# Feed forward's second projection by seven products of quarters, with accumulating transfers, and weights laid out tile by tile

## The reference, cut to what matters

```python
D_FF_2 = 4 * D_MODEL                       # 4096
def rmsnorm(x, g):
    xf = x.astype(jnp.float32)
    xf = xf * lax.rsqrt(jnp.mean(xf * xf, axis=-1, keepdims=True) + EPS)
    return (xf * g.astype(jnp.float32)).astype(x.dtype)

y = rmsnorm(h, pre_ff_g)                   # 512 x 1024
a = jnp.square(jax.nn.relu(y @ w_ff1))     # 512 x 4096, the hidden values
h = h + rmsnorm(a @ w_ff2, post_ff_g)      # 4096 x 1024 weights: the second projection
```

## Time and profile before

| | |
|---|---|
| median of 3 runs | 1729.72 us (1729.71 to 1730.04) |
| the profiled execution's own time | 1730.73 us |
| its span, first to last instruction | 1729.0 us |
| TensorE (PE) busy | 1715.3 us, 99% |
| VectorE (DVE) busy | 1209.1 us, 70% |
| ScalarE (ACT) busy | 820.2 us, 47% |
| GpSimd (POOL) busy | 46.4 us, 3% |
| moved by the 16 DMA engines | 181.36 MB, mean 105 GB/s |

### The profile page before, as it was taken

The page is one execution under the profiler, slowest core; times in us unless marked ns, Lnnn a source line. Parts: engine busy times, 40 slices in busy tenths (PEclk is TensorE's granted clock), DMA queues, the critical chain, the costliest instruction groups (busy, mean ns, idle before and its releaser), DMA issues.

```text
span 1729.0 us, 26320 instructions
## 1 busy us (share of the span) xinstructions
PE 1715.3 (99%) x10458; PEld 1497.2 (87%) x10458; DVE 1209.1 (70%) x1975; ACT 820.2 (47%) x1449; POOL 46.4 (3%) x103
## 2 busy tenths in 40 slices
PE   9999999999999999999999999999999999999998
PEld 8777788999999887777989999989888898999997
DVE  4588787777787735666877777868446876677776
ACT  4477744444445235664444444443565555333342
POOL 0212000000000000000000000000000000000000
PEclk9999999999999999999999999999999999999999
DMA  8343332333334232224133333352314224333331
GB/s 276 113 134 118 119 89 87 109 98 110 101 99 153 86 105 84 81 91 122 39 103 98 110 110 97 99 165 82 110 44 140 63 73 126 106 98 98 100 109 49
DMA packets 220125, 181.36 MB, mean 105 GB/s; under 512 B 9906, under 2 KB 178771, under 8 KB 220003
## 3 DMA queue, kind: packets, MB, share of 16 engines
q1 hardware_dynamic: 217954, 175.48, 33.1%
q0 software_dynamic: 2048, 4.20, 0.9%
HBM read 173.32 MB, written 7.38 MB: 105 GB/s over the span
## 4 chain that ended last, share of the span: by engine, by line
PE 93%; DVE 4%; ACT 1%; DMA 1%; issue 1%; POOL 0%; DVEq 0%; POOLq 0%
PE ps L733 29%; PE ps L734 28%; PE ps L735 28%; PE ps L1092 1%; PE ps L1137 1%; PE ps L1163 1%; PE ps L1112 1%; PE ps L1151 1%; DMA arena<-arena 1%; PE ps L987 1%; DVE wlo L1701 0%; DVE xl L1793 0%; PE ps L1102 0%; PE ps L972 0%; ACT whi L1321 0%
## 5 line engine op out<-in xcount | busy, mean ns | idle before, releaser
L1701 DVE TENSOR_TENSOR wlo<-raw,whi 128x1024 fp32r<-128x1024 f32 (+1 forms) x276 | 317.6, 1167 | 181.3 <-ACT whi L1321 181.0
L733 PE MATMUL ps<-xh,whi 128*128 128x256 f32 (+1 forms) x1016 | 332.4, 327 | 2.3 <-DVE xl L1793 2.3
L735 PE MATMUL ps<-xh,wlo 128*128 128x256 f32 (+1 forms) x1016 | 326.1, 321 | 0.0
L734 PE MATMUL ps<-xl,whi 128*128 128x256 f32 (+1 forms) x1016 | 325.9, 321 | 0.0
L1321 ACT ACTIVATE whi<-raw 128x1024 fp32r<-128x1024 f32 (+1 forms) x276 | 274.6, 1007 | 80.9 <-DMA raw<-in_w_ff 36.4
L733 PE MATMUL ps<-whi,hh 128*128 128x512 f32 x728 | 288.7, 397 | 1.4 <-DVE wlo L1701 1.3
L734 PE MATMUL ps<-wlo,hh 128*128 128x512 f32 x728 | 285.2, 392 | 0.0
L735 PE MATMUL ps<-whi,hl 128*128 128x512 f32 x728 | 283.6, 390 | 0.0
L733 PEld LDWEIGHTS ps<-xh,whi 128*128 128x128 f32 x1016 | 194.1, 191 | 25.8 <-issue 8.8
L735 PEld LDWEIGHTS ps<-xh,wlo 128*128 128x128 f32 x1016 | 194.1, 191 | 14.4
L734 PEld LDWEIGHTS ps<-xl,whi 128*128 128x128 f32 x1016 | 194.4, 191 | 12.2
(11 more groups left out here) (272 smaller groups left out, 2935.3 us busy)
## 6 DMA issues: line engine op xcount, KB each, us to landing
raw<-in_ffn_w_in SPq DMA_DIRECT2D x88, 512.0 KB, 3.8
raw<-in_w_ff SPq DMA_DIRECT2D x64, 512.0 KB, 4.2
raw<-in_ffn_w_out SPq DMA_DIRECT2D x44, 512.0 KB, 3.9
raw<-in_a_w_qkv SPq DMA_DIRECT2D x22, 512.0 KB, 5.5
raw<-in_w_in SPq DMA_DIRECT2D x20, 512.0 KB, 3.8
raw<-in_kv_w SPq DMA_DIRECT2D x16, 512.0 KB, 4.1
bias_skewed<-bias_rows SPq DMA_DIRECT2D x8, 640.0 KB
arena<-arena POOLq DMA_DIRECT2D x64, 64.0 KB, 2.7
```

Of the source, the lines that this page charges most:

```text
L733: e.matmul(o, ah, bh, start=start, stop=False, **more)
L734: e.matmul(o, ah, bl, start=False, stop=False, **more)
L735: return e.matmul(o, al, bh, start=False, stop=stop, **more)
L1701: e.tensor_tensor(lo[:, 0:n], src, f32(hi[:, 0:n]), ALU.subtract).then_inc(s.lo, 1)
```

## The change

1. **Seven products of quarters.** Groups 1 to 6 of the second projection (24 of the 32 hidden blocks) no longer make 16 `rows` steps. The 512 x 512 piece of hidden values and the 512 x 1024 piece of weights are cut in quarters, and seven products (`SEVEN`) are made instead of eight. Each is two "pieces" (token tiles t = 0, 1), a piece being six matmuls of 512 columns: 14 pieces and 84 matmuls per group. The products run as two chains of partial sums in PSUM, `a11 s2 s3 a22` and `a12`, `s1 s4`: a product may add to the bank in which the previous one of its chain stands.
2. **Eviction by ACT and accumulating transfers.** After every piece ACT copies the bank, with a sign, to one of four buffers `evicted` (in the space of `xh`/`xl`), and POOL issues a transfer that adds the 256 KB to the right quarter of `mb`. A piece's bank is waited for by PE, a buffer by ACT until the transfer of four pieces before has landed (`added`).
3. **Sums of weight quarters by transfers.** The right operands stand in the buffers of `x` (which is parked in DRAM meanwhile). Four loads of 512 KB come per group, and four accumulating transfers of 512 KB, issued by POOL from DRAM onto a buffer, turn one operand into the next (three in buffer `a`, one in `d`). ACT's split of the next operand waits for `right_sum`.
4. **Left operands.** The squared hidden values are stored whole (`hidden_words`) and DVE makes four sums of quarters per group (`left_sum`); seven operands are split (`left`, ACT then DVE) where four hidden blocks were split before.
5. **Places.** `FEED_PIECES` is "2212", 7 pieces per pair.
6. **Layout.** All weight tiles are laid out one behind the other before the launch (`tile_by_tile`), so each partition's row is one piece of 4 KB.
7. Around it: `x` goes to DRAM and back (`park`, `unpark`), the last gain vector has its own place (`gain`), and several semaphores are merged (no waits are added outside the last feed forward).

```diff
-FEED_PIECES = ["1111"] + ["2222"] * 13
+FEED_PIECES = ["1111"] + ["2212"] * 13
+SEVEN_FIRST, SEVEN_LAST = 1, 6
+SEVEN = [("a11", 0, True, 0, 0, 1), ("a12", 1, True, 0, 0, 1), ("s1", 1, True, 1, 1, -1), ("s4", 1, False, 0, 1, -1),
+         ("s2", 0, False, 0, 1, -1), ("s3", 0, False, 1, 1, -1), ("a22", 0, False, 1, 0, 1)]
...
+            elif what == "seven":
+                p, = arg
+                b, c = p.bank, slice(p.t * 128, p.t * 128 + 128)
+                wh, wl = self.weight(p.unit, 2)
+                lh, ll = self.left_parts(self.plan.entry_of[p.u])
+                w.wait_ge(s.lo, p.unit + 1)
+                w.wait_ge(s.left_lo, p.u + 1)
+                if p.before is None:
+                    w.wait_ge(*freed[b])
+                else:
+                    w.wait_ge(s.evicted, p.before + 1)
+                for k in (0, 1):
+                    m = mm3(e, ps[b][:], lh[:, k, c], ll[:, k, c], wh[:, k, :], wl[:, k, :], p.start and k == 0, k == 1,
+                            skip_group_check=True)
+                m.then_inc(s.rows, 1)
...
+            elif what == "left":
+                u, name, b, entry, (sem, value), free = arg
+                w.wait_ge(self.events[sem], value)
+                if free:
+                    w.wait_ge(s.rows, free)
+                e.activation(self.left_parts(entry)[0], self.left_source(name, b), ACT.Copy).then_inc(s.left_hi, 1)
+
+            elif what == "seven_post":
+                p, = arg
+                w.wait_ge(s.rows, p.value)
+                if p.sent >= 4:
+                    w.wait_ge(s.added[p.sent % 4], 16 * (p.sent // 4))
+                e.activation(self.evicted[p.sent % 4], ps[p.bank][:].rearrange("p (k c) -> p k c", k=2), ACT.Copy,
+                             scale=float(p.sign)).then_inc(s.evicted, 1)
...
+            elif what == "split" and self.plan.units[arg[0]][0] == "seven":
+                m, = arg
+                right = self.plan.units[m][1]
+                for buffer, chain, source in right.sums:
+                    if chain == "a":
+                        w.wait_ge(s.lo, m + 1)
+                    else:
+                        w.wait_ge(s.right[buffer], right.before)
+                    e.dma_start(self.x[:, buffer, :], self.row_tile(*source),
+                                accum_op=ALU.add).then_inc(s.right_sum[chain], 16)
+
+            elif what == "seven_post":
+                p, = arg
+                w.wait_ge(s.evicted, p.sent + 1)
+                w.wait_ge(s.mb, 16)
+                if p.earlier is not None:
+                    w.wait_ge(s.added[p.earlier % 4], 16 * (p.earlier // 4 + 1))
+                e.dma_start(self.mb[:, p.tile, p.nh * 512:p.nh * 512 + 512].rearrange("p (k c) -> p k c", k=2),
+                            self.evicted[p.sent % 4], accum_op=ALU.add).then_inc(s.added[p.sent % 4], 16)
...
         def weights(m):
...
+            e.dma_start(self.raw[:, m % RAW, :], ap["c_tiles"][m]).then_inc(s.raw[m % RAW], 16)
...
+            elif what == "park":
+                w.wait_ge(s.add, 8)
+                for t in range(4):
+                    e.dma_start(self.parked[t * 128:t * 128 + 128, :], self.x[:, t, :]).then_inc(s.x, 16)
```

More of the change, by code:

```diff
@@ L61, in __init__ @@
         self.kind, self.nh, self.t, self.bank, self.i = kind, nh, t, bank, i
-        self.norm, self.group, self.value = norm, group, None
+        self.norm, self.group, self.value, self.added = norm, group, None, None
+class Piece:
+    def __init__(self, u, unit, t, bank, start, before, value, tile, nh, sign, sent, earlier):
+        self.u, self.unit, self.t, self.bank, self.start, self.before, self.value = u, unit, t, bank, start, before, value
+        self.tile, self.nh, self.sign, self.sent, self.earlier = tile, nh, sign, sent, earlier
+class Right:
+    def __init__(self, buffer, need, sums=(), load=None):
+        self.buffer, self.need, self.sums, self.load, self.before = buffer, need, sums, load, None
 class Pair:
-    def __init__(self, kind, n, table, columns, blocks):
+    def __init__(self, kind, n, table, columns, blocks, first=None):
         self.kind, self.table, self.columns, self.blocks = kind, table, columns, blocks
@@ L339, in rows @@
             if last:
-                r.i = self.count(kind)
+                r.i, r.added = self.count(kind), self.added.get((t, nh))
             k = (row0 + k0) % 8
@@ L350, in rows @@
                 self.step("rows_post", r)
+                if kind == "f" and group == 0:
+                    self.plain_rows = r.value
             yield
@@ L494, in product @@
             self.read[{2: (1, 0), 7: (7, 0), 3: (6, pair.buf)}[j]] = pair.combined[j]
-            if j != 3:
-                self.step("combine", pair, j, self.counts["h"] - (j == 7) * pair.n_blocks)
+            if j != 3 and pair.kind == "relu":
+                self.step("combine", pair, j, pair.clear)
+            elif j != 3:
+                self.step("combine", pair, j, ("hl", self.counts["h"] - (j == 7) * pair.n_blocks))
+        if j == 5:
+            self.fifth = value
         if j in (2, 5, 4, 3):
@@ L1182, in tensor @@
                 w.wait_ge(s.la, 2)
[L1183 removed]
+                w.wait_ge(s.ident, 32)
                 w.wait_ge(*freed[b])
@@ L1314, in scalar @@
                     w.wait_ge(s.raw[tile % RAW], self.raw_at[tile])
+                elif kind == "seven":
+                    what, value = tile.need
+                    w.wait_ge(s.right[tile.buffer] if what == "load" else s.right_sum[what], value)
                 else:
@@ L1754, in vector @@
                 for i, k in enumerate(pair.blocks):
+                    if pair.kind == "relu":
+                        w.wait_ge(s.rows, self.plan.entry_free[3])
                     w.wait_ge(s.hh, pair.hidden[i] + 1)
@@ L2259, in sync @@
                 m, = arg
-                _, _, tile = self.plan.units[m]
+                kind, right, tile = self.plan.units[m]
+                if kind == "seven" and right.load is not None:
+                    w.wait_ge(s.hi, m + 1)
+                    w.wait_ge(s.lo, m + 1)
+                    rows_load(*right.load)
                 if tile is not None and tile + RAW < len(self.plan.tiles):
```

349 lines of the change are left out of this document (255 added, 94 removed).

## The result

The changed kernel takes **1896.41 us** (median of 4 runs), the kernel before 1729.88 in the same session: ratio 1.0965, interval 1.0946 to 1.0984. It is slower by 167 us where 1722.6 was forecast; the range ended at 1746. The profiled execution took 1899.86 us, its span is 1898.1 us.

What follows compares the result with a forecast made beforehand. PE's matmul time was taken as the bound. Matmuls -16.4, steady waits +3.0, entry +0.8 and the pairs' end +5.5 sum to -7.1 us: median 1722.6 us, forecast 1717 to 1726, whole range 1715 to 1746.

Steps and rivals of the forecast that it cites:

- Matmuls, -16.4: Six groups of the last feed forward: 12 of 96 matmuls of 512 columns leave each, 72 x 0.228 = -16.4 us.
- DVE comes to 33.2 us, ACT to 29.5: Work per steady group of 39.3 us: DVE from 30.1 to 33.2, ACT from 16.0 to 29.5; neither the bound.
- POOL issues a plain one in 0.49 us; 18 are 9 us, and at twice that still 18: POOL's issue of a group's 18 accumulating transfers, priced from plain ones: 9 to 18 us of 39.
- With 375 and 270 a group needs 32.6 us of engines: it fits: DMA engines per steady group: plain transfers at 375 GB/s, accumulating at 270, 32.6 us, 83% of 39.3.
- rival A: Accumulating makes DMA engines the bound, below 205 GB/s: 1746 us at 188 GB/s (cheaper half), more if doubled; chance 0.15.
- L is taken as 4.5, ends 2.7 and 7.9: Landing time of a sum of weight quarters, from POOL's issue: 4.5 us, between 2.7 and 7.9; up to 5.0 allowed.
- Rival B: Sums land late, L of about 5.0 or more: at 6.5 every steady group waits, 1742 us; chance 0.14.
- Steady waits +3.0, entry +0.8: PE's waits: 0.5 us in each of six steady groups, +3.0; where the pairs begin, +0.8, between -0.7 and +2.
- Where the pairs end, +5.5: End of group 6: wait for an eviction 2.7, third sum 0.8, clock 2.0; together 5.5 us, ends 0 and 12.
- the +2.0: Where the pairs end: PE's clock loss behind the forecast wait of 2.7 us, charged at +2.0 us.
- Layout: All other stages load weights in larger pieces: 0 us, since PE waits for no transfer there.
- case C: Nearly no change: L near 5, +1 us per group and +2 at the end, 1726 to 1733 us; chance 0.13.

Runs made afterwards that it cites:

- e3: The changed kernel without the 84 transfers that add to mb and the waits on them, sums of weight quarters kept, 64 places: 1729.71 us, ratio 0.9995 to the kernel before.
- e8: The changed kernel without the additions to mb and with dynamic_dma_scratch_size 1792 instead of 1024 (112 places): 1729.72 us, ratio 0.9996 to the kernel before.
- e2: The changed kernel with only dynamic_dma_scratch_size raised from 1024 to 1792 (112 places instead of 64): 1751.84 us.
- e7: The changed kernel with the 84 additions to mb made by POOL's own instruction and dynamic_dma_scratch_size 1792 (112 places): 1794.92 us.

## Why the prediction was wrong, step by step

- **"Matmuls, -16.4."** Right in kind: 72 fewer, 39.6 us of PE per group at full clock where additions are free.
- **"DVE comes to 33.2 us, ACT to 29.5."** Right, ACT 2 us too high: 33.4 and 27.2, and in the changed kernel itself 33.6 and 27.7. Neither was the bound.
- **"POOL issues a plain one in 0.49 us; 18 are 9 us, and at twice that still 18."** This is the step that failed. The issue took 1.21 us for an addition, and all issues 20.5 us per group, which alone would have passed. What I left out, and so put at nothing, is that POOL stands before the issue when what is in flight leaves the ring no room: 2.9 us and more before most additions with 64 places, and a group takes 70 us instead of 39.3. The bound from the rows was no bound at all: four plain transfers of 64 KB that go out within 1.96 us say nothing of what an accumulating one of 256 KB takes of the ring. The line that sets it, `dynamic_dma_scratch_size=1024`, stood in both kernels. This is 145 us of the 167, and none of my rivals holds it.
- **"With 375 and 270 a group needs 32.6 us of engines: it fits."** The second step that failed, in the direction of rival A's cheaper half. With room in the ring the engines were full and a group took 44.4 us, 4.0 above its plain twin (A's case of 188 GB/s: 41.9, waits beside). By the same sum as in the prediction, 5.77 MB in 44.4 - 11.2 us, the accumulating rate is some 174 GB/s, an estimate, and under A's threshold of 205. The runs agree with A in direction: 24 us, with whatever the larger number of packets costs in it, not the doubling to 53.9 us per group. I gave A 0.15; it deserved more, since all that spoke against it were rows of plain transfers.
- **"L is taken as 4.5, ends 2.7 and 7.9."** Without additions 5.4 us (e3) and 5.6 (e8), medians; with them at 112 places 7.3, in the changed kernel 7.0. Rival B's threshold of 5.0 was crossed even in the mildest case, and its chain is borne out: at 5.4 PE waited 0.3 to 1.0 us per group for a low part, at 7.3 (e2) 2.2 us, behind the 13 us of DVE's work that the prediction had counted. What B had too dear is the clock, 1.9 us for each such wait: in e2 the granted clock in the 5 us behind these five waits was 0.66 once and 1.00 four times.
- **"Steady waits +3.0, entry +0.8."** +4.9 over five groups with additions free.
- **"Where the pairs end, +5.5."** The chain was right, link by link (sum, split, low part, addition, two squares, hidden blocks, eviction), its size was not: 7.8 us of waits and 1.7 of clock, 9.5, since L was 5.3 and the sum was issued 4.9 us late. With 112 places 4.5 us of waits. As for the clock, no run shows the +2.0 as the price of a wait of 2.7 us, nor the 1.9 that rivals A and B charge for each wait. What the runs showed in its place: in the kernel before, behind the wait of 1.83 us, 17 intervals between matmuls of 256 columns (1378.57 to 1382.11) took 3.54 us, 1.5 more than at 0.120 each; in e3, behind the wait of 5.99 us, the 1.7 above. The row of 0.80 also begins 2.2 us after the wait of 1.83; in the 5 us right behind that wait (1377.75 to 1382.75) the granted clock was 0.66.
- **"Layout", 0.** Right, measured alone.

Together the errors besides the ring and the engines are 6 us (1.9 of steady waits, 4.0 at the end): they turn the forecast gain of 7 into nothing, with 1.3 us of the trace unassigned. That would have been my case C. The ring then added 145 us and accumulating, once the ring had room, 24.

## What to carry to other kernels

Before work is moved to transfers that POOL issues, ask for three things apart: what an issue takes, how many can be in flight (here `dynamic_dma_scratch_size` against what one transfer takes of it, by estimate 33 to 36 places for an accumulating one, at most 21 for its plain twin), and what rate the engines have for this kind. A trace that lacks the operation bounds none of them; measure one, or take the far end. Here, POOL standing for "issue" right before a transfer, and going on when the one before had landed, was the ring; raising one build number showed it in one run. Where such a line is seen elsewhere, the same run is worth making. And work moved from DVE to POOL was not free: it stretched DVE's own instructions, 45 of them from 33.4 to 48.7 us.

## What the runs showed that was not expected

- 8 more places, 1152 instead of 1024, brought 104 us, by letting a second accumulating transfer in.
- An accumulating transfer of 256 pieces of 1 KB fills, by estimate, 33 to 36 places, its plain twin at most 21, and goes out in 17 packets per engine against 5; its issue takes 1.21 against 0.72 us.
- With 64 places and no additions the third sum stood 4.4 to 5.0 us in five of the six groups, although only one transfer of 128 pieces was in flight; with 112 it did not (e8, e7). That a wider ring ends it is shown; why it is the third and not the fourth, which went out with one in flight as well, a count of places does not say, and it stays open.
- A POOL addition of 128 x 512 took 1.74 us beside DVE, where 1.29 was expected from the final norm, and DVE's 45 instructions of a group took 46% longer beside them.
